# Exact top-256 selection for seven query blocks at once, by bisection on the bits of the 256th value

## The chip, the core and the metric

The kernel runs on one core of one Trainium2 chip. The metric is the time of one execution on the device in microseconds (us). The engines of a core run their own instruction streams side by side and wait for each other through semaphores: TensorE (PE: matrix products and transposes), VectorE (DVE), ScalarE (ACT), GpSimd (POOL), and SyncE (SP), which here only starts DMA transfers.

## The reference, cut to what matters

The kernel is one step of a hybrid decoder layer. The stage of this change computes, for 1040 prompt rows (16 learned rows and 1024 of the prompt), a sparse attention in which every query sees only 256 keys that an indexer picks, and beside it a projection that has nothing to do with the attention:

```
sc = einsum('bqhd,bsd->bqhs', qi, ki_all) * (D_IDX ** -0.5)     # 8 indexer heads
score = einsum('bqhs,bqh->bqs', relu(sc), wi)
score = where(key_pos <= q_pos, score, -inf)
_, idx = lax.top_k(score, 256)                                  # ties: lower index first
valid = idx <= q_pos
s = where(valid, (q . k_sel) * HD_A ** -0.5, -inf);  p = softmax(s);  o = p @ v_sel
...
h = rms_norm(x, norm1_g) @ w_in          # columns of the RWKV branch and of two gates
pm = p_r + (prev - p_r) * rwkv_mu        # prev: the row before, in the same sequence
```

So for each query the 256 largest of up to 1040 scores are kept (fewer for the first rows), and the rest is masked with a large negative number before the softmax.

## The kernel before

`prompt_and_project` is one block of the program, from about 301 to 1196 us of the span. It does two things at once.

**Attention.** The queries are cut into nine blocks `QB` of up to 128 rows. A block sees `m` keys; the blocks come in the order m = 256, 1040 (a block of only 16 rows), 1024, 896, 768, 640, 512, 384, 128. For a block, TensorE makes the indexer's products in pieces of up to 512 keys and one of 8 heads (L351) into two PSUM buffers `PI`; ScalarE rectifies them into a ring `RL` (L462); VectorE multiplies by the head's weight and adds up (L558, L560) in `SCORE`. Then VectorE selects: 32 rounds of MAX8 (the 8 largest, L570) and MATCH_REPLACE8 (these 8 are overwritten with the number TAKEN, L572), and `choose` makes a mask from it (L578). For each of 8 heads of the block (72 heads in all) TensorE makes the scores (L371) in `PSC`, VectorE adds the mask and takes the maximum in one instruction with an accumulator (L591), ScalarE takes the exponential (L473), TensorE transposes (L387), ScalarE copies the transposed tiles back (L483), and TensorE multiplies with the values (L402). At a block's end `normalise` divides (L607), TensorE flips the rows (L412) and ScalarE places them (L499).

**Projection.** 90 units, each of eight products of 128 columns of the weights with 368 rows (L338; 30 column tiles t times 3), fill the gaps on TensorE: one after each eight indexer pieces, one in each head (in two halves, each behind a group of transposes), three at the end. ScalarE evacuates each unit (`evacuate`, L445 to L450), for t below 14 GpSimd blends each row with the row before it in five instructions (L527 to L535) and copies two columns aside, and SP stores the result.

**Order.** All of it is written out by hand, and each engine works its stream in order. While TensorE works the heads of block j, the indexer's pieces of block j+1 have been made ahead, and VectorE puts three rounds of the selection of block j+1 behind the peak of each of the heads 0 to 6 and the remaining 11 behind that of head 7. TensorE's scores of head u+1 wait for the peak of head u (semaphore `peaked`), since `PSC` holds one head; `PT` holds one group of four transposed tiles.

## Time and profile before

| | us |
|---|---|
| median of 3 runs (lowest, highest) | 3501.48 (3500.76, 3509.26) |
| the profiled execution: its own time | 3506.51 |
| its span, from the first to the last instruction | 3504.7 |
| TensorE busy, share of the span | 3101.3, 88% |
| VectorE busy, share of the span | 1703.0, 49% |
| ScalarE busy, share of the span | 855.1, 24% |
| mean granted TensorE clock, as a share of 2.4 GHz | 0.915 |

The profile gives for each engine when an instruction began and how long it took, and for idle time what ended it. "Busy" of TensorE counts pipelined products, so a product of 368 columns has a duration of some 500 ns while the next begins some 310 ns later; the distance of two starts is the cost, not the duration. Each fp32 product here has two records.

### The profile page before, as it was taken

The page shows a single profiled execution, that of the slowest core. Times are in us where ns is not written, and L with a number is a line of the kernel's source. Part 1 is how long each engine was busy: PE and PEld are TensorE (multiplying, and loading weights), DVE is VectorE, ACT ScalarE, POOL GpSimd, SP SyncE. Part 2 cuts the span into 40 slices and gives each one's busy share as a digit, 9 for nine tenths or more (in the row PEclk, how much of TensorE's full clock was granted, in tenths as well). Part 3 has the DMA queues.
Part 4 walks back from the last instruction along what each step waited for, and adds up shares of the span by engine and source line. Part 5 has one row for each costly group of instructions (what it writes and reads, how often), then busy time and mean ns, then how long its engine had stood idle before and what let it go on. Part 6 is the DMA issues. An engine that isn't in the chain of part 4 may idle for free. (4 is left out here: it accounts for less than half of the span.)

```text
span 3504.7 us, 46828 instructions
## 1 busy us (share of the span) xinstructions
PE 3101.3 (88%) x18312; PEld 1920.5 (55%) x18312; DVE 1703.0 (49%) x2842; ACT 855.1 (24%) x1897; POOL 329.0 (9%) x354
## 2 busy tenths in 40 slices
PE   6887877989999588679996999998899999999998
PEld 4553443655555332249992556655566666556665
DVE  2002888887761054374445799998722221121111
ACT  1112122322222123332221133201233331014420
POOL 0000211220000000000000022100143320000000
PEclk9998888999999898769996999998999889999999
DMA  3001010001111322300001622333354441352332
GB/s 132 11 10 36 35 40 29 26 32 47 42 50 53 105 73 60 113 21 4 4 5 40 205 98 104 110 112 112 120 180 132 136 142 42 104 166 97 108 111 77
DMA packets 87523, 273.94 MB, mean 78 GB/s; under 512 B 22616, under 2 KB 44216, under 8 KB 75408
## 3 DMA queue, kind: packets, MB, share of 16 engines
q1 hardware_dynamic: 75792, 220.49, 18.6%
q0 software_dynamic: 11520, 50.54, 4.5%
q8 instruction: 145, 2.38, 0.3%
q14 instruction: 66, 0.54, 0.0%
HBM read 238.47 MB, written 32.32 MB: 77 GB/s over the span
## 5 line engine op out<-in xcount | busy, mean ns | idle before, releaser
L1738 PE MATMUL tl_P<-tl_XN,tl_WU 128*128 128x368 f32 x2112 | 692.5, 490 | 5.8 <-DVE tl_XN L2086 5.8
L1738 PEld LDWEIGHTS tl_P<-tl_XN,tl_WU 128*128 128x128 f32 x2112 | 414.7, 198 | 266.6 <-issue 33.2
L1750 PE MATMUL tl_P<-tl_HT,tl_WD 128*128 128x368 f32 x1056 | 336.7, 479 | 0.0
L1750 PEld LDWEIGHTS tl_P<-tl_HT,tl_WD 128*128 128x128 f32 x1056 | 203.0, 193 | 127.8 <-issue 5.5
L338 PE MATMUL dp_RW<-xT,dp_W 128*128 128x368 f32 x784 | 267.1, 491 | 0.0
L570 DVE MAX8 dp_top<-dp_SCORE 16x8 f32<-16x1040 f32 (+6 forms) x224 | 211.2, 943 | 68.4 <-issue 68.4
L338 PE MATMUL dp_PSC<-xT,dp_W 128*128 128x368 f32 x656 | 228.6, 501 | 0.0
L572 DVE MATCH_REPLACE8 dp_SCORE<-dp_top,dp_SCORE 16x1040 f32<-16x1040 f32 (+6 forms) x224 | 207.0, 924 | 0.0
L149 PE MATMUL pa_PG<-pa_W,xT 128*128 128x402 f32 (+1 forms) x576 | 203.3, 515 | 1.6 <-PEq L34 1.6
L338 PEld LDWEIGHTS dp_RW<-xT,dp_W 128*128 128x128 f32 x784 | 149.1, 198 | 86.3 <-issue 13.5
L338 PEld LDWEIGHTS dp_PSC<-xT,dp_W 128*128 128x128 f32 x656 | 129.0, 204 | 79.5 <-issue 20.4
L371 PE MATMUL dp_PSC<-KT,QT 64*128 64x512 f32 (+5 forms) x240 | 103.8, 547 | 70.1 <-DVEq L597 70.1
L149 PEld LDWEIGHTS pa_PG<-pa_W,xT 128*128 128x128 f32 (+1 forms) x576 | 110.4, 193 | 90.6 <-issue 20.1
L1699 PE MATMUL tl_P<-tl_Z 128*128 128x368 f32 x384 | 129.1, 500 | 33.4 <-DMA tl_Z<-in_wb 16.9
L2033 DVE MAX8 tl_v<-tl_Z 128x8 f32<-128x4100 f32 x32 | 141.8, 4432 | 3.2 <-issue 1.4
L2036 DVE FIND_INDEX8 tl_i<-tl_v,tl_Z 128x8 uint32<-128x4100 f32 x32 | 141.5, 4423 | 0.3 <-issue 0.3
L2023 POOL DMA_INDIRECT tl_Z<-in_cache_kv,tl_PHT x128 | 122.3, 955 | 204.7 <-PE tl_P L1803 168.6
L2039 DVE MATCH_REPLACE8 tl_Z<-tl_v,tl_Z 128x4100 f32<-128x4100 f32 x32 | 141.2, 4414 | 0.0
L1868 ACT ACTIVATE tl_SQ<-tl_X 128x368 f32<-128x368 f32 x48 | 24.5, 509 | 462.5 <-PE tl_P L1683 191.0
L1699 PEld LDWEIGHTS tl_P<-tl_Z 128*128 128x128 f32 x384 | 77.4, 203 | 85.8 <-DMA tl_Z<-in_wb 18.6
L1711 PE MATMUL tl_P<-tl_HT,tl_Z 128*128 128x368 f32 x384 | 121.7, 472 | 0.9 <-issue 0.9
L2075 DVE TENSOR_TENSOR tl_X<-tl_X,tl_P 128x368 f32<-128x368 f32 x24 | 12.9, 538 | 224.1 <-PE tl_P L1750 223.5
(334 smaller groups left out, 4180.3 us busy)
## 6 DMA issues: line engine op xcount, KB each, us to landing
tl_WU<-in_wu SPq DMA_DIRECT2D x66, 1024.0 KB, 4.7
tl_WD<-in_wd SPq DMA_DIRECT2D x48, 704.0 KB, 3.9
dp_W<-in_w_rw SPq DMA_DIRECT2D x15, 1024.0 KB, 6.1
tl_Z<-in_wb SPq DMA_DIRECT2D x24, 512.0 KB, 3.7
tl_Z<-in_wo SPq DMA_DIRECT2D x24, 512.0 KB, 3.6
gates<-dp_PX SPq DMA_DIRECT2D x16, 552.0 KB, 2.9
tl_Z<-gates SPq DMA_DIRECT2D x48, 184.0 KB, 3.7
PM_dram<-dp_PMT SPq DMA_DIRECT2D x14, 552.0 KB, 3.0
```

The costliest lines, as they stand in the source:

```text
L149: last = pe.matmul(PG[0:n, c, 0:NC4], xT[:, k, r:r + n], W[:, k, NC4 * c:NC4 * c + NC4], start=k == 0, stop=k == KD - 1)
L338: last = pe.matmul(bank(u)[:, 0:w], W[:, t // 2 % 2, k, 128 * (t % 2):128 * (t % 2) + 128], xT[:, k, c:c + w], start=k == 0, stop=k == KD - 1)
L570: dve.max(top8[0:n, :], SCORE[0:n, 0:m])
L572: dve.match_replace(SCORE[0:n, 0:m], top8[0:n, :], SCORE[0:n, 0:m], TAKEN)
L1699: last = pe.matmul(out[:, 0:W], WM[:, i % 2, o:o + 128], YT[:, j, k, :], start=k == 0, stop=k == 3)
L1711: last = pe.matmul(out[:, 0:W], WM[:, i % 2, 128 * k:128 * k + 128], MT[:, k, :], start=k == 0, stop=k == KD - 1)
L1738: last = pe.matmul(out[:, 0:W], WU[:, i % 2, o:o + 128], XN[:, k, :], start=k == 0, stop=k == KD - 1)
L1750: last = pe.matmul(out[:, 0:W], WD[:, i % 3, 128 * e:128 * e + 128], HT[:, f, :], start=f == 0, stop=f == NF - 1)
L2023: pool.indirect_dma_start(out=KV[:, n % 16, t, :], out_offset=None, in_=I["cache_kv"], in_offset=bass.IndirectOffsetOnAxis(ap=PHT[:, 64 * ...
L2033: dve.max(v8[:, :], SC)
L2036: dve.max_index(i8[:, :], v8[:, :], SC)
L2039: dve.match_replace(SC, v8[:, :], SC, TAKEN)
```

## The change

- **All scores first.** The indexer's pieces of the seven blocks with m over 256 (104 pieces; the blocks with m = 256 and 128 need no selection, and their 16 pieces go) are made at the beginning, one after another, into one wide `SCORE` of 5264 columns. Four projection units stand among them, one after each 26 pieces.
- **Selection by bisection.** `bisect` finds the 256th largest value of each row exactly: first the sign, then 31 bits from the highest to the lowest. For each bit one instruction per block (`tally`, a TENSOR_SCALAR with compare and an accumulator that adds up) counts how many scores reach the trial value; three instructions on 128x7 elements update the seven blocks' bits together. A last tally counts the values above it. These are 33 tallies of seven instructions.
- **Ties by a running count.** `choose` marks the values equal to the 256th, numbers them with TENSOR_TENSOR_SCAN and keeps those for which there is room: five instructions and the causal one, where it was one and the causal one. It now stands behind the peak of head 4 of the block before; there are two `MASK` buffers.
- **Projection units.** TensorE's stream now holds 4 units among the pieces, 30 in a row behind the first scores (in this time VectorE bisects), then one in every head where m is at most 640 and in every second head where it is more: 56.
- **Heads.** The transposed tiles rotate through three PSUM buffers (`PT` and the two of `PI`, free by now) in place of one. `normalise` of a block stands behind the peak of head 0 of the next, its flip behind the scores of head 2.
- **Blending.** ScalarE evacuates a unit with t below 14 twice, scaled by 1-mu into `PMT` and by mu into `PX`; GpSimd only adds (two instructions). ScalarE writes the two columns of `SH`. SP's loads of the next weights stand ahead of the stores that they stood behind.

On VectorE, at the first block's heads, before: `ISA dp_P,dp_peak` is the peak of a head, the loop behind it the rounds of the next block's selection.

```order
 L591 ISA dp_P,dp_peak<-dp_PSC,dp_MASK 128x256
 L591 ISA dp_peak 128x1
 L595 TENSOR_SCALAR dp_npeak<-dp_peak 128x1
 L569 UNCONDITIONAL_BRANCH
 L570 MAX dp_top<-dp_SCORE 16x8
 L572 MATCH_REPLACE dp_SCORE<-dp_top,dp_SCORE 16x1040
 L569 REGISTER_ALU
 L569 COMPARE_AND_BRANCH
```

The same engine now, between the last piece of the indexer and the first peak: one bit of the bisection.

```order
 L569 TENSOR_SCALAR dp_EQ,dp_count<-dp_SCORE,dp_trial 16x1040
 L569 TENSOR_SCALAR dp_EQ,dp_count<-dp_SCORE,dp_trial 128x1024
 L569 TENSOR_SCALAR dp_EQ,dp_count<-dp_SCORE,dp_trial 128x896
 L569 TENSOR_SCALAR dp_EQ,dp_count<-dp_SCORE,dp_trial 128x768
 L569 TENSOR_SCALAR dp_EQ,dp_count<-dp_SCORE,dp_trial 128x640
 L569 TENSOR_SCALAR dp_EQ,dp_count<-dp_SCORE,dp_trial 128x512
 L569 TENSOR_SCALAR dp_EQ,dp_count<-dp_SCORE,dp_trial 128x384
 L584 TENSOR_SCALAR dp_step<-dp_count 128x7
 L586 TENSOR_TENSOR dp_bits<-dp_bits,dp_step 128x7
 L589 TENSOR_SCALAR dp_trial<-dp_bits 128x7
```

The rounds between the peaks are gone, and all of the selection stands in one run ahead of the first peak.

On TensorE, the change of block from m = 1040 to m = 1024 before: the last head, the pieces of the block after (m = 896) with their units, the flip, and the first two heads' scores.

```order
 L402 MATMUL dp_PO<-V,dp_PTS 16x64 x9
 L351 MATMUL dp_PI<-KIT,QIT 128x512 x8
 L338 MATMUL dp_PSC<-xT,dp_W 128x368 x8
 L351 MATMUL dp_PI<-KIT,QIT 128x384 x8
 L338 MATMUL dp_RW<-xT,dp_W 128x368 x8
 L412 MATMUL dp_PT<-ident,dp_OROW 128x16 x4
 L371 MATMUL dp_PSC<-KT,QT 128x512 x4
```

TensorE now, the end of the run of 30 units (two of them here) and the first head:

```order
 L347 MATMUL dp_RW<-xT,dp_W 128x368 x8
 L347 MATMUL dp_PSC<-xT,dp_W 128x368 x8
 L371 MATMUL dp_PSC<-KT,QT 128x256
 L394 MATMUL dp_PT<-ident,dp_P 128x128 x2
 L347 MATMUL dp_RW<-xT,dp_W 128x368 x8
 L408 MATMUL dp_PO<-V,dp_PTS 128x64 x2
```

The `L371` row here is the scores of head 1, which wait for the peak of head 0, and so for the whole bisection.

The diff, cut to its core:

```diff
...
+    SEL = [j for j, (_, _, m) in enumerate(QB) if m > TOPK]
+    NS = len(SEL)
...
-        EACH = 3
-        NR = 16
+        NR = 8
         RL = sb("RL", [128, NR, 512])
-        SCORE, MASK = sb("SCORE", [128, TP]), sb("MASK", [128, TP])
-        top8 = sb("top8", [128, 8])
+        SCORE = sb("SCORE", [128, sum(x for _, _, x in QB if x > TOPK)])
+        MASK = sb("MASK", [128, 2, TP])
+        EQ, ones = sb("EQ", [128, TP]), sb("ones", [128, TP])
+        bits, trial, step = (sb(n, [128, NS], I32) for n in ("bits", "trial", "step"))
+        count, over, room = (sb(n, [128, NS]) for n in ("count", "over", "room"))
...
-        DF = sb("DF", [128, R])
...
+        mu, rest = sb("mu", [128, NT]), sb("rest", [128, NT])
...
+        PTB = (PT0, PI[:, 0].rearrange("p (e n) -> p e n", e=4), PI[:, 1].rearrange("p (e n) -> p e n", e=4))
...
+        EVERY = 26
+        AMONG = len(all_pieces) // EVERY
+        fills = lambda u: int(QB[u // 8][2] <= 640 or u % 2)
+        AHEAD = NU - sum(fills(u) for u in range(NH))
+        units = [0] * AHEAD
+        for u in range(NH):
+            units += [int(u + 1 < NH and QB[(u + 1) // 8][2] > 1024)] * fills(u)
+        first_fill = [AHEAD + sum(fills(v) for v in range(u)) for u in range(NH + 1)]
+        of_head = lambda u: range(min(NU, first_fill[u]), min(NU, first_fill[u + 1]))
...
+                    if u % 6 == 5 and u // 6 + 2 < NU // 6:
+                        load(u // 6 + 2)
...
+                def dot(j, p):
                     i, n, m = QB[j]
-                    dots = dots0[j]
+                    c, w, h = pieces(j)[p]
+                    dots = dots0[j] + p
+                    if dots >= 2:
+                        pe.wait_ge(rectified, dots - 1)
+                    a = HD * (h % 2)
+                    pe.matmul(PI[0:n, dots % 2, 0:w], T["QIT"][a:a + HD, h // 2, 128 * i:128 * i + n],
+                              T["KIT"][a:a + HD, c:c + w], start=True, stop=True).then_inc(dotted, 1)
...
+                def values(u, fill):
+                    j, h = u // 8, u % 8
+                    i, n, m = QB[j]
+                    a, kv = HD * (h % 2), h // 4
+                    tiles = tile0[u]
+                    pe.wait_ge(expd, u + 1)
+                    for b, (t, k) in enumerate(groups(m)):
+                        if tiles >= 3:
+                            pe.wait_ge(untiled, tiles - 2)
+                        for e in range(k):
+                            w = min(128, m - 128 * (t + e))
+                            last = pe.transpose(PTB[tiles % 3][0:w, e, 0:n], P[0:n, u % 2, 128 * (t + e):128 * (t + e) + w],
+                                                ident[0:n, 0:n])
+                        last.then_inc(tiled, 1)
+                        tiles += 1
+                        if fill is not None and b < 2:
+                            half(fill, 4 * b)
+                    if fill is not None and len(groups(m)) == 1:
+                        half(fill, 4)
...
+                for d, (j, p) in enumerate(all_pieces):
+                    dot(j, p)
+                    if d % EVERY == EVERY - 1:
+                        half(d // EVERY, 0)
+                        half(d // EVERY, 4)
+                scores(0)
+                for f in range(AMONG, AHEAD):
+                    half(f, 0)
+                    half(f, 4)
+                for u in range(NH):
+                    j, h = u // 8, u % 8
+                    if u + 1 < NH:
+                        scores(u + 1)
+                    if h == 1 and j:
                         flip(j - 1)
-                    attention(j)
-                for u in fill:
-                    half(u, 0)
-                    half(u, 4)
+                    mine = of_head(u)
+                    values(u, mine[0] if mine else None)
                 flip(NQ - 1)
...
+                        act.activation(pm[:, c:c + w], ps[:, 0:w], ACT.Copy, scale=rest[:, t:t + 1])
+                        if c + w <= TP:
+                            act.activation(px[:, 1 + c:1 + c + w], ps[:, 0:w], ACT.Copy, scale=mu[:, t:t + 1])
...
+                for d, (j, p) in enumerate(all_pieces):
+                    rectify(j, p)
+                    if d % EVERY == EVERY - 1:
+                        evacuate(d // EVERY)
+                for f in range(AMONG, AHEAD):
+                    evacuate(f)
+                for u in range(NH):
+                    j, h = u // 8, u % 8
+                    exponential(u)
+                    if h == 1 and j:
                         place(j - 1)
-                    attention(j)
-                for f in fill:
-                    evacuate(f)
+                    untile(u)
+                    for f in of_head(u):
...
-                    pool.tensor_tensor(DF[:, 0:TP], px[:, 0:TP], px[:, 1:1 + TP], ALU.subtract)
-                    pool.tensor_tensor(dseq, seqs[:, :, 0:8], seqs[:, :, 1:9], ALU.subtract)
-                    pool.drain()
-                    pool.tensor_scalar(DF[:, :], DF[:, :], mu[:, t:t + 1], None, ALU.mult)
-                    pool.drain()
-                    if t >= 2:
-                        pool.wait_ge(pm_out[t % 2], 16 * (t // 2))
-                    pool.tensor_tensor(pm[:, 0:TP], DF[:, 0:TP], px[:, 1:1 + TP], ALU.add)
-                    pool.tensor_tensor(pm[:, TP:R].rearrange("p (b q) -> p b q", q=8), dseq,
-                                       seqs[:, :, 1:9], ALU.add)
-                    pool.tensor_copy(SH[:, t, 0:1], px[:, TP:TP + 1])
-                    pool.tensor_copy(SH[:, t, 1:], seqs[:, :, 8])
+                    pool.tensor_tensor(pm[:, 0:TP], pm[:, 0:TP], px[:, 0:TP], ALU.add)
+                    pool.tensor_tensor(later_rows, later_rows, seqs[:, :, 0:8], ALU.add)
                     pool.drain().then_inc(mixed, 1)
...
-                def take(j, rounds):
...
-                        dve.max(top8[0:n, :], SCORE[0:n, 0:m])
...
+                def tally(values, op, result):
+                    for x, j in enumerate(SEL):
+                        i, n, m = QB[j]
+                        dve.tensor_scalar(EQ[0:n, 0:m], scored_of(j), values(n, x), None, op, ALU.add,
+                                          accum_out=result[0:n, x:x + 1])
                         dve.drain()
-                        dve.match_replace(SCORE[0:n, 0:m], top8[0:n, :], SCORE[0:n, 0:m], TAKEN)
+
+                def bisect():
+                    dve.memset(count[:, :], 0.0)
+                    dve.memset(over[:, :], 0.0)
+                    dve.drain()
+                    tally(lambda n, x: 0.0, ALU.is_ge, count)
+                    dve.tensor_scalar(bits[:, :], count[:, :], float(TOPK), -1.0, ALU.is_ge, ALU.add)
+                    dve.drain()
+                    dve.tensor_scalar(trial[:, :], bits[:, :], 1 << 30, None, ALU.bitwise_xor)
+                    dve.drain()
+                    for b in range(30, -1, -1):
+                        tally(lambda n, x: trial[0:n, x:x + 1].bitcast(F32), ALU.is_ge, count)
+                        dve.tensor_scalar(step[:, :], count[:, :], float(TOPK), float(1 << b), ALU.is_ge, ALU.mult)
                         dve.drain()
+                        dve.tensor_tensor(bits[:, :], bits[:, :], step[:, :], ALU.bitwise_xor)
+                        dve.drain()
+                        if b:
+                            dve.tensor_scalar(trial[:, :], bits[:, :], 1 << (b - 1), None, ALU.bitwise_xor)
+                            dve.drain()
+                    tally(lambda n, x: bits[0:n, x:x + 1].bitcast(F32), ALU.is_gt, over)
+                    dve.tensor_scalar(room[:, :], over[:, :], -1.0, float(TOPK), ALU.mult, ALU.add)
...
                 def choose(j):
                     i, n, m = QB[j]
+                    mask = MASK[0:n, j % 2, 0:m]
                     if m > TOPK:
-                        dve.tensor_scalar(MASK[0:n, 0:m], SCORE[0:n, 0:m], TAKEN, -BIG, ALU.not_equal,
-                                          ALU.mult)
+                        x = SEL.index(j)
+                        least = bits[0:n, x:x + 1].bitcast(F32)
+                        dve.tensor_scalar(EQ[0:n, 0:m], scored_of(j), least, None, ALU.is_equal)
+                        dve.drain()
+                        dve.tensor_tensor_scan(mask, ones[0:n, 0:m], EQ[0:n, 0:m], 0.0, ALU.mult, ALU.add)
+                        dve.drain()
+                        dve.scalar_tensor_tensor(mask, mask, room[0:n, x:x + 1], EQ[0:n, 0:m], ALU.is_le, ALU.mult)
+                        dve.drain()
+                        dve.scalar_tensor_tensor(mask, scored_of(j), least, mask, ALU.is_gt, ALU.add)
+                        dve.drain()
+                        dve.tensor_scalar(mask, mask, BIG, -BIG, ALU.mult, ALU.add)
                     else:
-                        dve.memset(MASK[0:n, 0:m], 0.0)
+                        dve.memset(mask, 0.0)
                     dve.drain()
-                    causal(MASK, j, -BIG)
...
                 dve.wait_ge(later_in, 16)
-                weigh(0)
-                if QB[0][2] > TOPK:
-                    take(0, TOPK // 8)
+                dve.memset(ones[:, :], 1.0)
                 choose(0)
-                for j in range(NQ):
-                    ahead = j + 1 < NQ and QB[j + 1][2] > TOPK
-                    if j + 1 < NQ:
-                        weigh(j + 1)
-                    for h in range(8):
-                        peak_of(j, h)
-                        if ahead:
-                            take(j + 1, EACH if h < 7 else TOPK // 8 - 7 * EACH)
-                    normalise(j)
-                    if j + 1 < NQ:
+                for j, p in all_pieces:
+                    weigh(j, p)
+                bisect()
+                for u in range(NH):
+                    j, h = u // 8, u % 8
+                    peak_of(u)
+                    if h == 0 and j:
+                        normalise(j - 1)
+                    if h == 4 and j + 1 < NQ:
                         choose(j + 1)
+                normalise(NQ - 1)
 
 
 HALF = (PAST + QS) // 2
```

## Rows read from the trace of the kernel before

**Rows 1.** Windows: this stage. Stretch, length, busy us (count) by engine, clock, DMA share, GB/s.

```profile
301.00:1196.00 895.00, 779.83 (x3036) 466.68 (x3036) 601.58 (x1051) 220.68 (x511) 111.72 (x100) 0.92 0.11 40
```

**Rows 2.** Waits from 301 to 1196 us: who waited for whom, us, times, longest.

```profile
PE dp_PSC L371 <- DVEq L597: 70.1, 17, 17.1
```

**Rows 3.** Page, costliest groups: the two instructions of the removed selection.

```profile
L570 DVE MAX8 dp_top<-dp_SCORE 16x8 f32<-16x1040 f32 (+6 forms) x224 | 211.2, 943 | 68.4 <-issue 68.4
L572 DVE MATCH_REPLACE8 dp_SCORE<-dp_top,dp_SCORE 16x1040 f32<-16x1040 f32 (+6 forms) x224 | 207.0, 924 | 0.0
```

**Rows 4.** Timeline of VectorE: start us, length us, instruction (peak of one head).

```profile
662.02 1.23 DVE L591 CUSTOM_DVE_ANT_0 dp_P<-dp_PSC,dp_MASK 128x1024 f32<-128x1024 f32 x1 [0.34 <-issue]
663.17 0.08 DVE L591 DVE_READ_ACCUMULATOR2_ANT dp_peak<- 128x1 f32 x1
663.34 0.15 DVE L595 TENSOR_SCALAR dp_npeak<-dp_peak 128x1 f32<-128x1 f32 x1
```

**Rows 5.** Groups by shape on VectorE, whole span: busy us, mean ns of one.

```profile
L578 DVE TENSOR_SCALAR dp_MASK<-dp_SCORE 128x384 f32<-128x384 f32 x1 | 0.4, 360 | 0.1
L578 DVE TENSOR_SCALAR dp_MASK<-dp_SCORE 128x768 f32<-128x768 f32 x1 | 0.6, 560 | 0.1
L560 DVE SCALAR_TENSOR_TENSOR dp_SCORE<-dp_RL,WI,dp_SCORE 128x256 f32<-128x256 f32 x14 | 6.8, 485 | 3.2 <-ACT dp_RL L462 1.9
L2164 DVE TENSOR_REDUCE tl_st<-tl_P 32x1 f32<-32x320 f32 x16 | 7.7, 479 | 3.1 <-PE tl_P L1770 1.3
L963 DVE TENSOR_TENSOR_SCAN rf_T<-rf_keep,rf_E 128x384 f32<-128x384 f32 x8 | 7.7, 958 | 4.3 <-ACT rf_E L909 4.3
L591 DVE CUSTOM_DVE_ANT_0 dp_P<-dp_PSC,dp_MASK 128x384 f32<-128x384 f32 x8 | 4.5, 558 | 40.9 <-PE dp_PSC L371 40.7 <-issue 0.2
```

**Rows 6.** Timeline of TensorE and ScalarE: the first rectification; indexer products in pairs.

```profile
306.66 0.66 ACT L462 ACTIVATE dp_RL<-dp_PI 128x256 f32<-128x256 f32 x2 [10.85 <-DMA dp_sh<-in_shift]
431.64 1.61 PE L351 MATMUL dp_PI<-KIT,QIT 64*128 64x512 f32 x4 [0.20 <-ACT dp_RL L462]
433.45 1.61 PE L351 MATMUL dp_PI<-KIT,QIT 64*128 64x512 f32 x4 [0.20 <-ACT dp_RL L462]
692.41 0.66 ACT L462 ACTIVATE dp_RL<-dp_PI 128x256 f32<-128x256 f32 x2 [0.51 <-PE dp_PI L351]
693.58 0.66 ACT L462 ACTIVATE dp_RL<-dp_PI 128x256 f32<-128x256 f32 x2 [0.51 <-PE dp_PI L351]
```

**Rows 7.** Timeline of TensorE: the last projection unit and the last flip.

```profile
1184.75 5.11 PE L338 MATMUL dp_RW<-xT,dp_W 128*128 128x368 f32 x16
1189.70 0.60 PE L412 MATMUL dp_PT<-ident,dp_OROW 128*128 128x128 f32 x4
```

**Rows 8.** Timeline of TensorE: scores of heads, first and last of a run.

```profile
628.95 1.98 PE L371 MATMUL dp_PSC<-KT,QT 64*128 64x512 f32 x4
657.80 1.98 PE L371 MATMUL dp_PSC<-KT,QT 64*128 64x512 f32 x4
1003.01 1.12 PE L371 MATMUL dp_PSC<-KT,QT 64*128 64x512 f32 x2
1025.28 1.12 PE L371 MATMUL dp_PSC<-KT,QT 64*128 64x512 f32 x2
1069.24 0.91 PE L371 MATMUL dp_PSC<-KT,QT 64*128 64x384 f32 x2
1103.88 0.91 PE L371 MATMUL dp_PSC<-KT,QT 64*128 64x384 f32 x2
1129.45 0.48 PE L371 MATMUL dp_PSC<-KT,QT 64*128 64x128 f32 x2
1161.89 0.48 PE L371 MATMUL dp_PSC<-KT,QT 64*128 64x128 f32 x2
```

**Rows 9.** Groups by shape on ScalarE, 301 to 1196 us.

```profile
L483 ACT ACTIVATE dp_PTS<-dp_PT 128x512 f32<-128x512 f32 x48 | 28.7, 597 | 92.3 <-PE dp_PT L387 92.3
L445 ACT ACTIVATE dp_PX<-dp_RW 128x368 f32<-128x368 f32 x24 | 11.5, 479 | 94.2 <-PE dp_RW L338 94.2
```

More of the change, by code:

```diff
@@ L253, in prompt_and_project @@
         NQ = len(QB)
-        dots0 = [sum(8 * len(chunks(x)) for _, _, x in QB[:j]) for j in range(NQ + 1)]
-        tiles0 = [sum(8 * len(groups(x)) + 1 for _, _, x in QB[:j]) for j in range(NQ + 1)]
-        units = [0] * len(chunks(QB[0][2]))
-        for j in range(NQ):
-            if j + 1 < NQ:
-                units += [0] * len(chunks(QB[j + 1][2]))
-            units += [int(QB[j][2] > 1024)] * 8
-        units = (units + [0] * NU)[:NU]
+        NH = 8 * NQ
+        pieces = lambda j: [(c, w, h) for c, w in chunks(QB[j][2]) for h in range(8)] \
+            if QB[j][2] > TOPK else []
+        dots0 = [sum(len(pieces(x)) for x in range(j)) for j in range(NQ + 1)]
+        first_col = [sum(QB[x][2] for x in SEL if x < j) for j in range(NQ)]
+        all_pieces = [(j, p) for j in SEL for p in range(len(pieces(j)))]
+        tile0, flip0, tiles = [], [], 0
+        for u in range(NH):
+            if u % 8 == 1 and u > 8:
+                flip0.append(tiles)
+                tiles += 1
+            tile0.append(tiles)
+            tiles += len(groups(QB[u // 8][2]))
+        flip0.append(tiles)
+        EVERY = 26
[7 more added lines that the diff above has]
+        of_head = lambda u: range(min(NU, first_fill[u]), min(NU, first_fill[u + 1]))
         second, turn = [], 1
@@ L269, in prompt_and_project @@
         first_wide = units.index(1)
-        after_wide = max(u for u in range(NU) if units[u]) + 1
         bank = lambda u: PSC[:, 1024:1536] if second[u] else RW[:, :]
@@ L323, in _ @@
             def _(pe):
-                fill = iter(range(NU))
                 def half(u, k0):
@@ new lines, in flip @@
+                    for e in range(4):
+                        last = pe.transpose(PTB[flip0[j] % 3][:, e, 0:n], OROW[0:n, 128 * e:128 * e + 128], ident[0:n, 0:n])
+                    last.then_inc(tiled, 1)
+                def values(u, fill):
+                    j, h = u // 8, u % 8
+                    i, n, m = QB[j]
+                    a, kv = HD * (h % 2), h // 4
+                    tiles = tile0[u]
[7 more added lines that the diff above has]
+                                                ident[0:n, 0:n])
+                        last.then_inc(tiled, 1)
+                        tiles += 1
+                        if fill is not None and b < 2:
+                            half(fill, 4 * b)
+                    if fill is not None and len(groups(m)) == 1:
+                        half(fill, 4)
+                    pe.wait_ge(untiled, tiles)
+                    if h == 0 and j > 0:
+                        pe.wait_ge(normed, j)
+                    for t in range(-(-m // 128)):
+                        w = min(128, m - 128 * t)
+                        v = 128 * kv + a
+                        last = pe.matmul(PO[0:n, HD * h:HD * h + HD], PTS[0:w, u % 2, t, 0:n],
+                                         T["V"][0:w, t, v:v + HD], start=t == 0, stop=128 * t + w == m)
+                    last.then_inc(summed, 1)
@@ L567, in take @@
[L567 to L573 removed]
+                    c, w, h = pieces(j)[p]
+                    dots = dots0[j] + p
+                    dve.wait_ge(rectified, dots + 1)
+                    rl, wi = RL[0:n, dots % NR, 0:w], T["WI"][0:n, i, h:h + 1]
@@ new lines, in weigh, with scored_of @@
+                    score = SCORE[0:n, first_col[j] + c:first_col[j] + c + w]
+                    if h == 0:
+                        dve.tensor_scalar(score, rl, wi, None, ALU.mult)
+                    else:
+                        dve.scalar_tensor_tensor(score, rl, wi, score, ALU.mult, ALU.add)
+                    dve.drain().then_inc(weighted, 1)
+                    if p == len(pieces(j)) - 1:
+                        causal(SCORE[:, first_col[j]:first_col[j] + m], j, LOW)
+                def scored_of(j):
+                    i, n, m = QB[j]
+                    return SCORE[0:n, first_col[j]:first_col[j] + m]
```

228 lines of the change are left out of this document (70 added, 158 removed).

## The prediction

> **What bounds the kernel now.** I read the windows of this stage first. It lasts 895 us; TensorE is busy in 780 of them, VectorE in 602, at a granted clock of 0.92 [rows 1]. So TensorE is the bound as a sum, and VectorE is so by turns: the waits show TensorE's scores behind a peak for 70.1 us in 17 pieces, the longest 17.1 [rows 2]. These stand at the starts of blocks and behind head 7 with its eleven rounds. The removed selection is 211.2 + 207.0 us busy plus 68.4 us of loop branches, 487 us on VectorE [rows 3], nearly all of it under TensorE's work. The reader should keep this in mind: it is long, but only some 70 us of it are waited for. What matters is how long the new one is and what lies beside it, since it stands in one run, ahead of the first peak.
>
> **The change, part by part.** The stage has three stretches now, and I take each by the engine that ends it.
>
> *Stretch 1, pieces of the indexer.* ScalarE can begin when the first small loads have landed, at 306.7 us [rows 6], and has one small instruction more there (0.3). Pieces run in pairs through the two `PI` buffers: 433.45 - 431.64 = 1.81 us for two of 512 columns, 693.58 - 692.41 = 1.17 for two of 256, so 0.905 and 0.585 each [rows 6]. VectorE keeps pace: its instruction for 256 columns takes 0.485 us [rows 5], with a gap of 0.1 as much as the pair allows, and 0.85 by one column per cycle for 512. Of the 104 pieces 64 have 512 columns (57.9 us), 16 have 384 (0.745 each between the two, 11.9), 8 have 256 (4.7), 8 have 128 and 8 have 16 (some 0.42 and 0.3 by the same slope, 5.8): 80.3. Four projection units at 4.95 us (1189.70 - 1184.75 [rows 7]) and 0.5 each to get the pairs running again: 22. Slow clock at the first ones 2, the last piece and its causal instruction 1.5. It ends at 306.7 + 0.3 + 80.3 + 22 + 2 + 1.5 = 413 us. Ends: 400 to 425.
>
> *Stretch 2, the bisection.* 33 tallies of seven instructions over 5264 columns. No row shows this instruction. From below: a TENSOR_SCALAR without accumulator takes 360 ns for 384 columns and 560 for 768, 0.52 ns per column over 0.16 fixed [rows 5]. In the middle: the instruction of the peaks, with accumulator, takes 558 ns for 384 and 1.23 us for 1024, 1.04 ns per column over 0.16 [rows 4, 5]; the reduction over 320 columns takes 479 ns, the same slope if its fixed part is 0.15. From above: the scan takes 958 ns for 384, 2.08 ns per column over 0.16. I take 1.04, since what comes nearest in kind is what accumulates. The fixed part: 0.16, 0.06 more for the trial value read from SBUF (485 ns for 256 columns leaves 0.22 [rows 5]), and 0.09 until the next can start: 662.02 to 663.34 for 1.23, with the accumulator's own read in between [rows 4]. So one tally is 7 x 0.31 + 5264 x 1.042 ns = 2.17 + 5.49 = 7.66 us, 33 are 252 (0.4 less for the one with a constant). Some 98 small instructions at 0.15 + 0.09 [rows 4]: 23.5. Together 276 us, to 689. Beside it TensorE has 30 units, 30 x 4.95 = 149 us, to some 564; ScalarE's double evacuation of 2 x 0.48 us [rows 9] fits under 4.95 each. Then TensorE stands for some 125 us before the scores of head 1. By the slope of 0.52 the bisection is 33 x 5264 x 0.521 = 90.5 us shorter; by that of 2.08, 181 longer.
>
> The Trainium skill speaks against this edit: SBUF — State Buffer, "Who interferes with whom", counts `tensor_scalar` among what can use both port pairs, but "not the form that also writes out its accumulator". By that rule the tally has no double rate, which is the 276 us above; if one leaves the accumulator out of account, the plain rows would promise 186.
>
> *Stretch 3, 72 heads with 56 units.* Nothing but peaks and masks is left on VectorE, so a head costs what TensorE needs. The distances of scores in steady runs give that: with a unit, 1024 keys (657.80 - 628.95)/3 = 9.62 us, 512 keys 22.27/3 = 7.42, 384 keys 34.64/5 = 6.93, 128 keys 32.44/5 = 6.49 [rows 8]; between 1024 and 512 that is 0.55 per 128 keys. Eight heads each: 640 keys 63.8, 512 59.4, 384 55.4, 128 51.9, 256 (at 6.7) 53.6. Of 1040 (taken as 1024), 1024, 896 (9.07) and 768 (8.52), four heads each with a unit: 147.3; and four without, at the mean of 9.21 less 4.95, plus some 1.2 of waiting, since no unit covers ScalarE's copy of the last tiles (597 ns [rows 9] and its semaphores both ways): 5.46 x 16 = 87. Sum 518.4. The first block's heads carry units with t below 14, evacuated twice ahead of the next exponential: 8 x 1.2 = 10 (0 if it is hidden). Eight flips 5. TensorE comes out of a long wait with a slow clock: 3. `choose` is long now: for 1024 columns two TENSOR_SCALARs at half a cycle per column (1.4 us), the scan (2.3), two of three inputs (2.6), causal and gaps (0.9) give 7.2, between two peaks; what a head without unit doesn't cover is 4 us at the largest block, 2.5, 2, 1 and 0.5 at its neighbours: 10. Sum 546, ends 520 (no extras) and 590. The stretch ends at 689 + 546 = 1235; the last `normalise` and flip have no unit over them any more, 2: 1237, against 1190.3 for the last flip before [rows 7]. What follows is the same.
>
> *The rest.* GpSimd's three instructions fewer per tile, SP's loads ahead of the stores and the three buffers of tiles take away nothing that TensorE waited for much; the 16 pieces not made any more (some 8 us) are already out of stretch 1, the stalls of 70 us at peaks out of stretch 3. I cost them at nothing beyond that.
>
> **The sum.** 1237 - 1190 = +47 us. The profiled execution took 3506.5 us, its span 3504.7, and stands 5 us over the median; added to its own time it gives 3553.5, and to the median 3548.5. I say 3548, 1.3% slower. The cross-check: the wait of 125 us beside the bisection alone exceeds the 70 us of waits that go; what is gained on top is the slow clock and some 20 us of waits at ScalarE.
>
> **The rivals.**
>
> 1. *The tally runs at two columns per cycle* (the other side). Place: stretch 2. Price: 90.5 us less, so 3548 - 90 = 3458. It decides from the point where the bisection is 47 us shorter, which is 0.77 ns per column. For it: the opcode is the same TENSOR_SCALAR, and both operands are in SBUF in fp32, as in the rows at 0.52. Against it: the accumulating rows, all at 1.04. Even then VectorE ends the stretch (186 against 149 us). Chance 0.13.
>
> 2. *TensorE's heads don't reach their pace.* The 16 heads without a unit are short bursts with waits between, and the clock was 0.92 in a stage with fewer of them [rows 1]; if their 4.3 us of work go at 1.2 GHz, they take up to twice that, 16 x 3 = 48 us, and the waits after `choose` grow: 3596. For it: the many waits in them. Against: the pace of the runs with units was even. Chance 0.06.
>
> 3. *The selection costs what the old one cost outside of cover, no more*: gaps between tallies smaller than 0.09, no wait for evacuation, `choose` covered: 276 - 20, 546 - 25, nothing else: 3503. This is no change. Chance 0.06.
>
> 4. *The accumulator needs two cycles per column*, as the scan does: 3548 + 181 = 3729. Chance 0.03.
>
> **How the numbers follow.** The forecast has 0.72 with its own range of 3512 to 3580 (bisection 255 to 295, stretch 3 from 525 to 570, stretch 1 by 8 either way, not all at the same end). The range to 8 in 10 takes in rival 3 and the lower half of rival 2: 3500 to 3590. Out of it are rivals 1 and 4 and little else. A measurement of this kernel can tell 0.3%, some 10 us, from no change. Faster: rival 1 and a rest, 0.15. Same: rival 3, 0.06. Slower: 0.79.
>
> **What would show it.** In the changed kernel's trace: tallies of 1024 columns at 1.29 us (at 0.75 rival 1 holds, at 2.35 rival 4); the first peak at about 689 us of the span; TensorE idle for 125 us before it, the run of 30 units at 4.95 us each; the first head's scores behind a wait for VectorE; heads of 1024 keys by turns at 9.6 and 5.5 us (by rival 2 at 9.6 and 8 or more); `choose` with a scan of 2.3 us; the last flip at 1237. The prediction is wrong if the bisection ends before 640 us, or if stretch 3 takes less than 500 us.

## The result and the profile after

The changed kernel takes 3567.4 us (median of 4 runs, 3563.3 to 3571.8) against 3503.2 (4 runs on the same chip): 1.0181 times as long, interval 1.0160 to 1.0202. The forecast was 3548 with a range of 3500 to 3590. Other runs below were made on other chips of the same type, where the kernel before takes up to 3524 us; so each is given as a ratio to the kernel before on its own chip, and places inside an execution are compared by one event, the start of the last flip (`OROW`) of this stage: 1189.70 us before [rows 7], 1250.62 after.

The windows of the changed kernel by the three stretches of the forecast and the rest (columns as in [rows 1]):

```profile
301.00:423.00 122.00, 108.31 (x259) 42.23 (x260) 68.57 (x116) 53.01 (x116) 3.23 (x4) 0.72 0.07 23
423.00:706.00 283.00, 155.00 (x496) 94.67 (x494) 252.47 (x560) 37.67 (x102) 24.80 (x20) 0.78 0.10 39
706.00:1251.00 545.00, 516.42 (x2250) 328.54 (x2250) 114.01 (x276) 154.58 (x347) 7.25 (x6) 0.96 0.11 38
1251.00:3562.00 2311.00, 2079.59 (x14532) 1313.67 (x14530) 1064.91 (x1683) 591.13 (x1296) 209.37 (x231) 0.91 0.30 97
```

Read the first two busy columns of the second row: TensorE has 155 us of work in 283, VectorE (third) 252. The stage ends 60.9 us later than before; the rest takes 2311 us, where it took about 2315. The whole difference arises in this stage.

The waits of the changed kernel from 301 to 1260 us, TensorE's rows (us, times, longest), where [rows 2] stood:

```profile
PE dp_PSC L371 <- DVEq L626: 128.2, 1, 128.2
PE dp_PO L408 <- ACTq L493: 16.4, 20, 1.0
PE dp_PI L359 <- ACT dp_RL L469: 12.9, 30, 4.8
```

Seventeen waits of 70.1 us together became one of 128.2. Its place in TensorE's timeline of the changed kernel (the last unit ahead, the first score that waits, and the last flip):

```profile
572.89 5.11 PE L347 MATMUL dp_PSC<-xT,dp_W 128*128 128x368 f32 x16
706.20 1.22 PE L371 MATMUL dp_PSC<-KT,QT 64*128 64x256 f32 x2 [128.21 <-DVEq L626]
...
1250.62 0.66 PE L380 MATMUL dp_PI<-ident,dp_OROW 128*128 128x128 f32 x4 [1.09 <-DVEq L640]
```

The groups by shape on VectorE in the changed kernel (busy us, mean ns of one), which answer to the bounds of [rows 5] and replace [rows 3]:

```profile
L569 DVE TENSOR_SCALAR_CACHE_REDUCE dp_EQ<-dp_SCORE,dp_trial 128x1024 f32<-128x1024 f32 x31 | 39.6, 1279 | 3.0
L569 DVE TENSOR_SCALAR_CACHE_REDUCE dp_EQ<-dp_SCORE,dp_trial 128x384 f32<-128x384 f32 x31 | 19.0, 613 | 3.0
L584 DVE TENSOR_SCALAR dp_step<-dp_count 128x7 int32<-128x7 f32 x31 | 7.9, 254 | 2.4
L603 DVE TENSOR_TENSOR_SCAN dp_MASK<-dp_ones,dp_EQ 128x1024 f32<-128x1024 f32 x1 | 2.3, 2291 | 0.1
```

From 384 to 1024 columns the tally grows by 1279 - 613 = 666 ns, which is 1.04 ns per column. The instruction appears under a name of its own, not as TENSOR_SCALAR as rival 1 assumed. The page has all of it in one row, `x217 | 215.7, 994`, about as much busy time as one of the two removed instructions had [rows 3]. VectorE works less than before, and TensorE waits more.

### The profile page after: what moved, and what is told of

Read it like the earlier page. It is cut to its first block and busy times, and to the rows that moved or that the text cites. A ratio compares the mean times of both kernels' runs of the same rounds, so it can differ in the third digit from the quotient of the medians.

```text
span 3561.9 us, 46008 instructions
## 1 busy us (share of the span) xinstructions
PE 3098.9 (87%) x18280; PEld 1920.2 (54%) x18280; DVE 1536.6 (43%) x2742; ACT 879.5 (25%) x1952; POOL 253.0 (7%) x284
## 5 line engine op out<-in xcount | busy, mean ns | idle before, releaser
L347 PE MATMUL dp_RW<-xT,dp_W 128*128 128x368 f32 x752 | 253.6, 490 | 0.0
L569 DVE TENSOR_SCALAR_CACHE_REDUCE dp_EQ<-dp_SCORE,dp_trial 16x1040 f32<-16x1040 f32 (+6 forms) x217 | 215.7, 994 | 21.8 <-issue 1.3
L620 DVE CUSTOM_DVE_ANT_0 dp_P<-dp_PSC,dp_MASK 128x256 f32<-128x256 f32 (+8 forms) x72 | 58.4, 811 | 362.3 <-PE dp_PSC L371 361.6
L371 PE MATMUL dp_PSC<-KT,QT 64*128 64x512 f32 (+5 forms) x240 | 102.3, 541 | 128.2 <-DVEq L626 128.2
L149 PEld LDWEIGHTS pa_PG<-pa_W,xT 128*128 128x128 f32 (+1 forms) x576 | 111.1, 195 | 90.8 <-issue 21.5
L371 PEld LDWEIGHTS dp_PSC<-KT,QT 64*128 64x128 f32 (+1 forms) x240 | 36.4, 174 | 164.9 <-DVEq L626 128.8
```

The source lines that it names most:

```text
L149: last = pe.matmul(PG[0:n, c, 0:NC4], xT[:, k, r:r + n], W[:, k, NC4 * c:NC4 * c + NC4], start=k == 0, stop=k == KD - 1)
L347: last = pe.matmul(bank(u)[:, 0:w], W[:, t // 2 % 2, k, 128 * (t % 2):128 * (t % 2) + 128], xT[:, k, c:c + w], start=k == 0, stop=k == KD - 1)
L371: last = pe.matmul(PSC[0:n, c:c + w], T["QT"][a:a + HD, h // 2, 128 * i:128 * i + n], T["KT"][a:a + HD, kv, c:c + w], start=True, stop=True)
L569: dve.tensor_scalar(EQ[0:n, 0:m], scored_of(j), values(n, x), None, op, ALU.add, accum_out=result[0:n, x:x + 1])
```

## The experiments

The theory after the result: the loss is TensorE's wait for the bisection, whose length is set by one column per cycle of the accumulating tally, and what the new order of units gives or takes is small beside it. The rivals: the time sits in the heads that lost their unit, or in the pieces made alone at a slow clock. Every change below is to the changed kernel unless it says otherwise. "Flip" is how far the last flip moved against 1250.62 us.

### Fewer bits

```diff
-                    for b in range(30, -1, -1):
+                    for b in range(30, 18, -1):    # x2_bits22: range(30, 8, -1)
```

> The changed kernel with the bisection stopped after 12 of its 31 bits (19 bits are left out, so that the threshold is coarse). Theory A, the loss is TensorE's wait for the bisection: a bit costs 283/33 = 8.6 us on VectorE, so the bisection shrinks from 283 to 120 us and ends under the 149 us of the 30 units; the wait of 128 us goes and no more than that: 3567 - 128 = 3439 us, 64 below the kernel before. Rival B, the loss is in the heads (slow clock in heads without a unit, `choose`, double evacuation) and the wait is given back there: less than 100 us come off, 3470 or more. Rival C, it is VectorE's sum: 163 us come off, 3404.

> The changed kernel with the bisection stopped after 22 of its 31 bits (the lowest nine are left out). Theory A: 9 x 8.6 = 77 us come off and VectorE still ends the stretch: 3490 us, with 51 us of wait left on TensorE. If the price is not one to one with the bits (rival B), the time stays above 3510.

With 12 bits of 31 the time is 0.9823 of the kernel before (0.9799 to 0.9846), flip -122.8 us. With 22 it is 0.9935 (0.9918 to 0.9953), flip -75.9. The waits of the one with 22 bits:

```profile
PE dp_PSC L371 <- DVEq L626: 53.8, 1, 53.8
```

Nine bits take 74.4 us off this wait, 8.3 each, and the flip follows one to one. With 12 bits the wait has no row any more: the units ahead now end last, and the flip moves by the whole wait at most (128.2), not by 19 x 8.3 = 158. So the wait is on the path in full, and with the bisection covered the changed kernel is faster than the one before.

### The tally without accumulator

```diff
-                        dve.tensor_scalar(EQ[0:n, 0:m], scored_of(j), values(n, x), None, op, ALU.add,
-                                          accum_out=result[0:n, x:x + 1])
+                        dve.tensor_scalar(EQ[0:n, 0:m], scored_of(j), values(n, x), None, op)
...
-                    dve.memset(count[:, :], 0.0)
+                    dve.memset(count[:, :], 300.0)
...
-                        dve.tensor_scalar(step[:, :], count[:, :], float(TOPK), float(1 << b), ALU.is_ge, ALU.mult)
+                        dve.tensor_scalar(step[:, :], count[:, :], float(TOPK), 0.0, ALU.is_ge, ALU.mult)
```

Nothing is counted in this version: the counts are set once and no bit is ever taken, so it leaves out the selection and keeps only its instructions.

> The changed kernel with the tally's accumulator left out (the compare writes its result as before, nothing is counted, and the thresholds stay at zero): 231 instructions at the price of a plain TENSOR_SCALAR. Theory A with one column per cycle due to the accumulator: 33 x 5264 x 0.52 ns = 90 us and 231 x 0.08 = 18 us of accumulator reads come off, 283 - 108 = 175 us, still over the 149 of the units: 3567 - 108 = 3459 us, tallies of 1024 columns at 0.75 us. If the compare itself or the pointer kept it at one column per cycle, only the reads go: 3549. GpSimd's additions (2.4 us per tile, ten tiles) may delay some: up to 15 us more.

0.9929 (0.9910 to 0.9949), flip -82.3. The tally of this kernel by shape, first the 31 of the loop, then the one behind it:

```profile
L569 DVE TENSOR_SCALAR dp_EQ<-dp_SCORE,dp_trial 128x1024 f32<-128x1024 f32 x31 | 26.9, 869 | 2.4
L569 DVE TENSOR_SCALAR dp_EQ<-dp_SCORE,dp_bits 128x1024 f32<-128x1024 f32 x1 | 0.8, 753 | 0.1
```

The same data, shape and operation take 753 ns without the accumulator and 1279 with it. The accumulator alone is what makes the difference between rival 1 and the forecast. The bisection is 80.4 us shorter and not the 108 expected, for two reasons. The 31 in the loop average 869 and not 753: the longest lasted 2778 ns, and the long ones stand beside GpSimd's additions (2.0 to 2.8 us each). By the means of all seven shapes this is 0.6 us per bit, 18.5 in all. And the accumulator's read costs far less than its 0.08 us: a tally begins 0.10 us after the end of the one before with it and 0.08 without, so 231 reads gave some 5 us, not 18. The accumulating form shows nothing of the kind: its 217 records lie between 612 ns (384 columns) and 1285 (1040).

### More units ahead

```diff
-        fills = lambda u: int(QB[u // 8][2] <= 640 or u % 2)
+        fills = lambda u: int(u % 2 if QB[u // 8][2] <= 640 else u % 4 == 3)
```

> The changed kernel with 62 projection units ahead of the heads in place of 34 (a unit in every second head up to 640 keys and in every fourth above, so 28 in the heads), selection whole and exact. Theory A: the run of 58 units takes 58 x 4.95 = 287 us and covers the bisection of 283; TensorE's wait of 128 goes; the 28 heads that lose their unit wait some 1.2 us each for ScalarE's copy, 34 us, and TensorE's slow clock in heads without a unit may cost 15 to 45 more: 3567 - 128 + 34 + 15..45 = 3488 to 3518, middle 3500. Rival D: heads without a unit lose as much as the wait was worth (slow clock in most of them): 3530 or more. If they cost nothing at all: 3439.

1.0033 (1.0022 to 1.0045), flip -53.6. The windows of this kernel's bisection and heads:

```profile
414.00:697.00 283.00, 283.00 (x911) 173.31 (x910) 252.50 (x560) 55.54 (x146) 32.06 (x26) 0.99 0.19 70
697.00:1200.00 503.00, 459.86 (x1837) 289.38 (x1835) 114.38 (x278) 137.48 (x304) 0.00 (x0) 0.81 0.08 25
```

and its timeline of TensorE, scores of heads: the first of 1040 keys, five of 1024 (a unit follows the fourth of these), and the first of 640:

```profile
743.85 2.66 PE L371 MATMUL dp_PSC<-KT,QT 64*16 64x512 f32 x6
...
818.94 1.98 PE L371 MATMUL dp_PSC<-KT,QT 64*128 64x512 f32 x4
824.90 1.98 PE L371 MATMUL dp_PSC<-KT,QT 64*128 64x512 f32 x4
832.07 3.78 PE L371 MATMUL dp_PSC<-KT,QT 64*128 64x512 f32 x4
842.06 3.78 PE L371 MATMUL dp_PSC<-KT,QT 64*128 64x512 f32 x4
855.89 1.98 PE L371 MATMUL dp_PSC<-KT,QT 64*128 64x512 f32 x4
...
1004.78 2.50 PE L371 MATMUL dp_PSC<-KT,QT 64*128 64x512 f32 x4
```

The first of 1040 and of 640 keys in the changed kernel:

```profile
759.66 1.93 PE L371 MATMUL dp_PSC<-KT,QT 64*16 64x512 f32 x6
1010.21 1.34 PE L371 MATMUL dp_PSC<-KT,QT 64*128 64x512 f32 x4
```

The wait is gone: TensorE is busy for all of the 283 us at a clock of 0.99. But 28 units left the heads, 139 us at 4.95, and the heads (707.57 to 1197.02) are only 55 us shorter than after the change (706.20 to 1250.62). So of the 4.95 us that each of them lost, 3 came back as slower work or waits, and 2 were gained. The clock says where: 0.81 in place of 0.96. The same four products take 1.98 us or 3.78, and heads without a unit stand 5.96 us apart in one case (818.94 to 824.90) and 9.99 in the other (832.07 to 842.06). This is what rival 2 of the forecast described. The mean of 3 us hides a split. The four blocks of 1040 to 768 keys, now with three of four heads bare, lost eight units and still took 260.9 us (743.85 to 1004.78) for 250.6 (759.66 to 1010.21): 10 us more for 40 us less of units. The other five blocks, with every second head bare, lost twenty units and became 65 us shorter, 3.3 us for each. So it is the large blocks that did not bear it. A version that thins only the small ones was not run, but for four heads at the end. What a bare head costs with one of two bare in the large blocks, the next experiment shows.

### All heads with their unit

```diff
-        fills = lambda u: int(QB[u // 8][2] <= 640 or u % 2)
+        fills = lambda u: 1
```

> The changed kernel with a projection unit in every one of the 72 heads and only 18 ahead, 14 of them beside the bisection. Theory A with the heads' price from x4_ahead (a head that loses its unit of 4.95 us gets only 2.3 us shorter, since waits and the slow clock take 2.6): the stretch of the bisection stays 283, TensorE waits 207 there, and the 16 heads that get a unit lengthen by 2.3 to 3.7 us each: 37 to 59 us more, ratio 1.029 to 1.035. If a unit in a head without one is wholly covered by its waits: 1.018; if heads paid nothing for losing units: 16 x 4.95 = 79 us, 1.041.

1.0293 (1.0273 to 1.0312), flip +42.4. Its waits:

```profile
PE dp_PSC L371 <- DVEq L626: 207.0, 1, 207.0
```

The wait grows by 78.8 us, the 16 units that no longer fill it (16 x 4.95 = 79.2), and the heads with them (704.36 to 1292.97) are only 44 us longer, not 79. So in the changed kernel a head without a unit loses 2.2 of its 4.95 us to slower work or waits, and taking the unit away brings the remaining 2.8 (44.2 / 16). This part of the change helps, and the loss isn't there.

### Units among the pieces

```diff
-        EVERY = 26
+        EVERY = 105    # y1_none_among; y4_eight_among: EVERY = 13
```

> The changed kernel with no projection unit among the indexer's pieces: all 34 that stand ahead of the heads stand in the run beside the bisection. Theory A, VectorE's bisection ends that stretch: 34 x 4.95 = 168 us still lies under 283, so the four units cost nothing there, and the pieces end some 20 us earlier: ratio to the kernel before 1.018 - 0.006 = 1.012. If TensorE's slow clock among the pieces, with even less to do, takes the gain: 1.016 to 1.018. Rival E, the four units were free among the pieces (TensorE waited there anyway): unchanged, 1.018.

> The changed kernel with eight projection units among the indexer's pieces, one behind each 13, in place of four. After y1_none_among, where the clock stood at half over all pieces and a pair of 512 columns took 2.76 us for 1.81: theory F, units among the pieces keep the clock up. Four more units cost 20 us, of which the faster pieces give back some 10 (the slices of slow clock that are left in the changed kernel: pairs at 2.76 in about half of the pieces): the pieces end at 430 to 435 us for 423, the time is 8 to 12 us longer, ratio 1.020 to 1.022. Rival G, the clock among the pieces doesn't depend on the units: 20 us longer, pieces end at 443, ratio 1.024.

With none: 1.0193 (1.0176 to 1.0210), flip +2.7, no change against the 1.0181 of the changed kernel. With eight: 1.0255 (1.0236 to 1.0275), flip +24.9. Windows around 340 to 380 us, first the changed kernel:

```profile
340.00:380.00 40.00, 35.94 (x100) 15.04 (x99) 28.28 (x44) 21.93 (x44) 0.00 (x0) 0.98 0.00 1
```

then the one with no unit among the pieces:

```profile
340.00:380.00 40.00, 37.47 (x64) 14.85 (x60) 21.56 (x33) 15.87 (x30) 0.00 (x0) 0.50 0.00 1
```

and the latter's timeline, two pairs of 512-column pieces:

```profile
338.90 2.56 PE L359 MATMUL dp_PI<-KIT,QIT 64*128 64x512 f32 x4 [0.20 <-ACT dp_RL L469]
341.66 2.56 PE L359 MATMUL dp_PI<-KIT,QIT 64*128 64x512 f32 x4 [0.20 <-ACT dp_RL L469]
```

In this execution the pieces alone never leave the lower clock: 0.50, and 2.76 us per pair instead of 1.81 [rows 6]. That isn't so in all: in x4_ahead, with the same pieces ahead, a pair of the first block goes from 2.56 to 1.71 us at about 312, and the first unit begins at 324.3. So a unit isn't needed for the rise. In these 40 us VectorE (third column) gets 33 instructions to do in place of 44. The units cost nothing there, as the pieces are faster beside them: `bisect` begins at 425.1 without them and at 422.9 with them. (Only three of the four, 15 us, stand ahead of it: the fourth follows the last piece.) Four more don't pay again: it begins at 443.7, 20.8 later for 4 x 4.95, where theory F gave 7 to 12. The clock is 0.82 in the mean there, with four 0.72 and with none 0.50, but TensorE also stands idle for 18.5 us until `bisect` begins, where it was 13.7: what the clock gave, some 4 us, the waits behind the units took. The time, 1.0255, fits the price of rival G; its reason, that the clock doesn't depend on the units, isn't what the windows show.

### The kernel before without its selection

```diff
-                        if ahead:
-                            take(j + 1, EACH if h < 7 else TOPK // 8 - 7 * EACH)
```

> The kernel before with its selection left out: the MAX8 and MATCH_REPLACE8 rounds are not made (every key is masked alike, so that the attention's numbers are not the reference's), all else as it was. It shows what the old selection cost on the path. Theory A: the 70 us of waits of TensorE for the peaks go, and some slow clock with them: 3503 - 70 to 90, ratio 0.974 to 0.980. If the old selection was as exposed as its 487 us on VectorE suggest, much less: below 0.95. If it was hidden wholly: 1.000.

0.9739 (0.9723 to 0.9755), its last flip at 1098.94, 90.8 us before that of [rows 7]. (The one `take` ahead of the first block is out too; it never ran, since that block has only 256 keys.) Its waits show

```profile
PE dp_PSC L371 <- DVEq L597: 10.6, 9, 1.6
```

so 59.5 of the 90.8 stood as waits in [rows 2], and 31 us did not. The old selection was dearer on the path than its row of waits, yet of its 487 us on VectorE over 80% were hidden. Of the new one's 283 us, 128 are not. With the new one hidden as well (12 bits) the flip is at 1127.84, 28.9 us after this kernel's; that is what is left for `choose`, the bare heads and the pieces' own stretch together. No run divides it up.

### A faster bisection: three blocks on ScalarE

```diff
+                        act.activation(RL[0:n].rearrange("p r c -> p (r c)")[:, at:at + m], SCORE[0:n, first_col[j]:first_col[j] + m],
+                                       ACT.Sign, bias=trial[0:n, q:q + 1].bitcast(F32), scale=-1.0,
+                                       accum_out=less[0:n, q - ND:q - ND + 1])
...
+                        dve.tensor_tensor(count[:, ND:], offset[:, :], less[:, :], ALU.subtract)
```

The blocks of 1024, 896 and 384 keys are counted by ScalarE, as a sum of signs of trial minus score, with one evacuation of a unit behind each bit; VectorE keeps the other four. The count decides rightly as long as at most one score of a row equals the trial value.

> The changed kernel with the tallies of three of the seven blocks (1024, 896 and 384 columns) made on ScalarE in the 31 bits: Sign of the trial value less the score, with its accumulator; the comparison of their count is made right for at most one score equal to a trial value. A bit takes VectorE four tallies (4 x 0.31 + 2960 x 1.042 ns = 4.3 us) and four small instructions (0.9), ScalarE three (3 x 0.58 + 2304 x 0.833 ns = 3.7) and an evacuation of 1 to 1.5: 5.5 to 6 us per bit with the semaphores, 31 of them and two whole tallies 186 to 202 us against 283. Theory A, it is the bisection's length that TensorE waits for: 81 to 97 us come off, and TensorE's 30 units, now paced by ScalarE, still fit: ratio 0.991 to 0.995. If evacuations and tallies get in each other's way on ScalarE: 1.00 to 1.01.

0.9947 (0.9928 to 0.9965), flip -86.8. The bisection takes 204 us in place of 283. VectorE's timeline of this kernel within one bit:

```profile
503.01 0.16 DVE L609 TENSOR_TENSOR dp_count<-dp_offset,dp_less 128x3 f32<-128x3 f32 x1
504.04 1.28 DVE L589 TENSOR_SCALAR_CACHE_REDUCE dp_EQ<-dp_SCORE,dp_trial 16x1040 f32<-16x1040 f32 x1
...
508.36 2.02 DVE L609 TENSOR_TENSOR dp_count<-dp_offset,dp_less 128x3 f32<-128x3 f32 x1
```

and GpSimd's:

```profile
508.34 2.03 POOL L553 TENSOR_TENSOR dp_PMT<-dp_PMT,dp_PX 128x1040 f32<-128x1040 f32 x1 [15.65 <-ACTq L466]
```

A bit is 5.3 us where nothing disturbs it. A wait of 23.2 us is left, so four more units fit ahead of the heads, taken from those of the last block:

```diff
-        fills = lambda u: int(QB[u // 8][2] <= 640 or u % 2)
+        fills = lambda u: int(128 < QB[u // 8][2] <= 640 or u % 2)
```

> z1_split (three blocks' tallies on ScalarE) with four units moved from every second head of the last block (128 keys) to the run beside the bisection, so 38 ahead. In z1_split TensorE still waited 23 us there, which is 4.7 units. A head that loses its unit gets 2.3 us shorter (x4_ahead): 4 x 2.3 = 9 us less, ratio 0.9947 - 0.0026 = 0.992. If ScalarE's evacuations of the four lengthen the bisection by as much: 0.9947. If the heads of 128 keys, the shortest, lose all of it to waits and slow clock: 0.9947 to 0.996.

0.9887 (0.9870 to 0.9903), flip -104.9, and 44.0 us before that of [rows 7]: this version beats both kernels. Its windows:

```profile
423.00:620.00 197.00, 177.95 (x544) 104.03 (x544) 172.66 (x393) 128.82 (x298) 27.04 (x22) 0.97 0.17 64
620.00:1146.00 526.00, 498.27 (x2189) 316.91 (x2188) 115.88 (x278) 150.91 (x337) 4.96 (x4) 0.95 0.11 37
```

The clock during the bisection is 0.97, where the change has 0.78. The expectation was 0.992, so the gain was undersized. Of the further 18.1 us against the split alone, 14.3 lie in the last block (from its first scores to the last flip 45.3 us, 1100.41 to 1145.70, for 59.6, 1104.23 to 1163.80). A head there gave 3.6 of its 4.95 us where 2.3 was expected; 2.9 us lie in the blocks before, and the heads begin 1.0 earlier. No row of a wait of TensorE for VectorE's peaks is left.

## Why the prediction was right, and where its sum was off

1. *Bisection at one column per cycle, 276 us.* Right: 1.04 ns per column as chosen, 283 us measured (422.9 to 706.2). The 7 us missing are the small instructions: two of the three per bit last 254 and 243 ns in the mean, not 150. Three of these 61 lasted 1.07, 1.85 and 2.32 us beside GpSimd's additions, the rest take 0.17. "A tally of 1024 at 1.29" was 1.279. The bound from above, the scan's rate, is itself confirmed for the scan (2291 ns) and doesn't hold for the tally.
2. *Stretch 1 ends at 413.* 422.9 in this execution. In executions of kernels whose code is the same up to there it was 414.0 (more units ahead), 416.9 and 418.2 (the two with ScalarE), 418.1 (no accumulator), 418.9 (22 bits), 420.3 (12 bits) and 422.9 (all heads with a unit). The step that failed is "slow clock at the first ones 2": the clock is 0.72 in this stretch, a pair takes 2.76 us while it is low, and how long it is low varies by up to 9 us. A second error hid part of it. The sum holds four units, but only three lie ahead of the bisection, since the fourth stands behind the last piece:

```profile
421.11 7.66 PE L347 MATMUL dp_PSC<-xT,dp_W 128*128 128x368 f32 x16
422.89 0.06 DVE L574 MEMSET dp_count<- 128x7 f32 x1
```

The first line is the fourth unit, the second the beginning of `bisect`. Without its 5.5 us the sum gives 407.5, so the slow clock was sized too small by 6.5 to 15.4 us, and not by the 1 to 10 that the ends show.
3. *TensorE waits for 125 us.* Right: 128.2. Both ends of the wait came late, the units at 578 for 564 and the bisection at 706 for 689, so their distance held.
4. *Stretch 3, 546 us, plus 2 for the last flip.* 544.4 (706.20 to 1250.62). That it is so near is in part luck: two terms missed in opposite directions. `choose` cost TensorE nothing, not 10: no head's scores wait for it. The slow clock cost more than 3: in the four largest blocks five heads with their unit took 12.4 to 14.0 us, one of 1024 keys 12.9 (855.97 to 868.91), where their neighbours took 9.4 to 10.0, some 17 us in all. The other terms, 535 together, came to 527. The pace was near the forecast: these are scores in the changed kernel, with a head without a unit between the first two and one with a unit between the last two.

```profile
834.07 1.98 PE L371 MATMUL dp_PSC<-KT,QT 64*128 64x512 f32 x4
840.04 1.98 PE L371 MATMUL dp_PSC<-KT,QT 64*128 64x512 f32 x4
850.01 1.98 PE L371 MATMUL dp_PSC<-KT,QT 64*128 64x512 f32 x4
```

5.97 bare (5.46 forecast) and 9.97 with a unit (9.62).
5. *The sum.* +47 forecast, +60.9 measured: +10 from stretch 1, +7 from the bisection, -4 from stretch 3. The rest of the kernel, costed at nothing, gave 4 back. Stretches 1 and 3 were forecast nearer than some of their own terms, by the cancellations in 2 and 4; the main term, the bisection, was right by itself.
6. *The rivals.* Rival 1 had the right price: without the accumulator the bisection is 80.4 us shorter (418.1 to 621.0), where 90.5 was given, and the kernel is faster than before. Its condition doesn't hold. Rival 2 is real: 2.2 us for each of 16 bare heads here (it gave 3), of which the forecast's paces held 0.8 (4.95 less the 4.16 between 9.62 and 5.46), and 3.0 in the mean for each head stripped further. Rivals 3 and 4 are out by the 1.0181 and the 1279 ns.

What "SBUF — State Buffer" of the Trainium skill says in "Who interferes with whom", that the accumulating form isn't among those with both port pairs, agrees with both halves of the tally experiment: the rate (753 against 1279 ns), and that only the form without accumulator was held up beside GpSimd.

Left open: the doubled evacuation and the order of SP's loads were not undone alone; by the waits at L478 (10.8 us in the stage, 1.1 the longest) the former can be worth some 10 us, near the 0.3% that a measurement can tell. Nor was it tried whether ScalarE can count with any number of equal scores.

## What to carry to other kernels

Busy time that falls can still lose: ask of a selection, a sort or a search not how long it is, but how much independent work stands beside it in the order of the queues. An operation that is spread in slices between the peaks hid over 80% of 487 us, and one in a single run hid only 155 of 283. Before filling such a gap with work taken from elsewhere, count what that work was doing there: here the clock fell without it, and moving 139 us of it brought 55. It matters where it is taken from: twenty units out of the small blocks brought 65 us, and eight out of the large ones cost 10.

## What the runs showed of the hardware

- The accumulating form of an element-wise instruction on VectorE costs 1.04 ns per fp32 column where the plain form costs 0.52; its accumulator's read is an instruction of its own of 0.08 us, yet the next tally begins 0.10 us after the end of the one before, against 0.08 without it. A trial value read from SBUF in place of a constant adds 58 to 60 ns (1279 against 1221 in the changed kernel, 753 against 693 without accumulator).
- An instruction of 3 columns on VectorE lasted 2.02 us beside a GpSimd addition of 1040 columns (2.03 us, begun 0.02 earlier); the same one took 0.16 a bit before. In a chain of dependent small instructions this is paid in full.
- TensorE with short fp32 products and a wait of 0.2 us per pair stayed at half its clock for all of 122 us in y1_none_among, busy 109 of them. With units among the pieces it was at 0.72 in the mean (four) and 0.82 (eight); in x4_ahead it rose before the first unit. "Busy" in the windows is therefore no sign of a fast clock; the granted clock stands in its own column.
- ScalarE's sign of 1024 columns with accumulator takes 1.15 us and 0.19 for the read, less than the 1.28 of VectorE's tally: it can count too.
